# Scan decays of a two-layer hybrid step: running sums spread over the partitions by DMA and a minimum of two differences, in place of two triangular products

## The reference, cut to what matters

```
cs = jnp.cumsum((dt * A).reshape(b, nc, T, H), axis=2)
decay_in = jnp.exp(jnp.where(causal, cs[:, :, :, None, :] - cs[:, :, None, :, :], -jnp.inf))
y_diag = jnp.einsum('bclsh,bcshp->bclhp', cb * decay_in, xdt)
states = jnp.einsum('bclhn,bclhp->bchpn', Bh * jnp.exp(cs[:, :, -1:, :] - cs)[..., None], xdt)
```

## Time and profile before

| | |
|---|---|
| median of 3 runs | 1350.33 us (1347.05 to 1352.32) |
| the profiled execution | 1345.9 us, its span 1343.4 us |
| mean granted clock of TensorE | 0.974 of full |
| PE / DVE / ACT / POOL busy | 1214.7 / 457.9 / 328.4 / 210.2 us |

### The profile page before, as it was taken

The page is one execution under the profiler, slowest core; times in us unless marked ns, Lnnn a source line. Parts: engine busy times, 40 slices in busy tenths (PEclk is TensorE's granted clock), DMA queues, the critical chain, the costliest instruction groups (busy, mean ns, idle before and its releaser), DMA issues.

```text
span 1343.4 us, 16757 instructions
## 1 busy us (share of the span) xinstructions
PE 1214.7 (90%) x6414; PEld 682.4 (51%) x6414; DVE 457.9 (34%) x1019; ACT 328.4 (24%) x840; POOL 210.2 (16%) x269
## 2 busy tenths in 40 slices
PE   4999998999999999969999788999888969989787
PEld 2456654555545554446555444753455546555443
DVE  1442078543237760361111114122364351111114
ACT  4212364200022300231111113213353231111112
POOL 1000022200123601011122102052001011111201
PEclk9998999999999999969999999999999969999999
DMA  9995920576920128269999998860313479999994
GB/s 342 376 380 190 340 67 1 210 263 216 366 92 1 63 73 329 79 246 392 419 418 419 420 410 321 275 63 3 141 63 116 178 258 413 418 419 420 419 404 186
DMA packets 94306, 342.83 MB, mean 255 GB/s; under 512 B 12654, under 2 KB 16468, under 8 KB 69409
## 3 DMA queue, kind: packets, MB, share of 16 engines
q1 hardware_dynamic: 73680, 309.47, 58.9%
q0 software_dynamic: 13664, 25.47, 6.9%
q10 hardware_dynamic: 6897, 6.97, 1.5%
HBM read 340.05 MB, written 28.43 MB: 274 GB/s over the span
## 4 chain that ended last, share of the span: by engine, by line
PE 67%; DMA 18%; DVE 6%; issue 4%; ACT 2%; POOL 2%; SPq 0%; ACTq 0%; DVEq 0%; POOLq 0%
PE bank L888 59%; DMA ring<-in_moe_w_down_dram 9%; PE bank L892 5%; DMA ring<-in_moe_w_up_dram 3%; PE bank L919 2%; DMA expert_rows<-arena,scr 2%; DMA ring<-in_ev_w_in_dram 2%; DMA arena<-expert_rows 1%; DMA ring<-in_w_ada_dram 1%; POOL ring L2742 1%; POOL hT L2745 1%; ACT ring L2029 1%; POOL arena L2745 0%; PE bank L965 0%; DVE arena L2609 0%
## 5 line engine op out<-in xcount | busy, mean ns | idle before, releaser
L888 PE MATMUL bank<-ring,arena 128*64 128x256 f32 (+3 forms) x2592 | 428.7, 434 | 38.2 <-DMA ring<-in_moe_w_up_dram 14.4
L888 PEld LDWEIGHTS bank<-ring,arena 128*64 128x64 f32 (+1 forms) x2592 | 214.7, 145 | 218.7 <-issue 113.6
L888 PE MATMUL bank<-hT,ring 128*128 128x384 f32 (+4 forms) x960 | 299.1, 469 | 3.0 <-DVE hT L2158 1.7
L888 PEld LDWEIGHTS bank<-hT,ring 128*128 128x128 f32 (+1 forms) x960 | 176.4, 191 | 122.3 <-issue 16.0
L888 PE MATMUL bank<-arena 128*64 128x256 f32 (+8 forms) x856 | 138.7, 400 | 16.1 <-DVE arena L2500 8.1
L888 PEld LDWEIGHTS bank<-arena 128*64 128x64 f32 (+4 forms) x856 | 67.7, 150 | 67.6 <-issue 40.9
L2549 DVE TENSOR_TENSOR hT<-hT,bank 128x256 f32<-128x256 f32 x32 | 13.5, 421 | 249.9 <-ACT hT L1920 249.9
L1920 ACT ACTIVATE hT<-bank 128x256 f32<-128x256 f32 x32 | 12.3, 384 | 238.7 <-PE bank L888 238.7
L892 PEld LDWEIGHTS bank<-cst,hT 128*128 128x128 f32 x368 | 49.3, 195 | 41.9 <-issue 38.7
L892 PE MATMUL bank<-cst,hT 128*128 128x128 f32 x368 | 61.9, 305 | 6.5 <-DVE arena L2520 4.3
L2554 DVE COPY arena<-bank 128x512 f32<-128x512 f32 x32 | 22.1, 692 | 124.1 <-PE bank L888 104.6
(11 more groups left out here) (323 smaller groups left out, 1159.9 us busy)
## 6 DMA issues: line engine op xcount, KB each, us to landing
ring<-in_moe_w_up_dram SPq DMA_DIRECT2D x28, 2048.0 KB, 21.1
ring<-in_moe_w_down_dram SPq DMA_DIRECT2D x26, 2048.0 KB, 19.7
ring<-in_w_ada_dram SPq DMA_DIRECT2D x24, 2048.0 KB, 15.7
ring<-in_moe_w_gate_dram SPq DMA_DIRECT2D x24, 2048.0 KB, 22.5
ring<-in_ev_w_in_dram SPq DMA_DIRECT2D x10, 2048.0 KB, 12.7
arena<-in_moe_w_gate_dram SPq DMA_DIRECT2D x8, 2048.0 KB, 16.3
arena<-in_moe_w_down_dram SPq DMA_DIRECT2D x6, 2048.0 KB, 21.8
ring<-in_ev_w_out_dram SPq DMA_DIRECT2D x4, 2048.0 KB, 17.4
```

The lines of the kernel that those rows point to most:

```text
L888: return nc.tensor.matmul(out, lhsT, rhs, start=start, stop=stop_, skip_group_check=True)
```

## The change

The two triangular products, their bank E and the scaled triangles are gone. In their place:

- After z chunk 3 and token_tiles(0), PE makes the running sums once, six small products that put 16 heads on 16 partitions: for each direction d and chunk t, dta against upto or since (banks "cs"). ACT copies them to runs_out and issues two DMAs on its queue to a DRAM tensor runs (3, 2, 16, 128).
- SP, behind the four copies of zeros, issues for each of the 12 steps a load that spreads the sums of four heads and both directions over all 128 partitions (128 x 2 x 512 numbers, 512 KB each), into three buffers in turn. The first waits for the two DMAs and for xbc, the next two for the last use of the lent slot's block (z chunk 7), each later one for the step that last used its buffer.
- ACT copies minus the running sum at the partition's own position to `here` (3 small copies beside wt). ramps(n) is now eight ACT instructions in place that add `here` to the spread sums; each is the difference cs[l] - cs[s] of one direction and head.
- DVE takes the smaller of the two directions' differences (L2231's place in the order), and ACT the exponential of that, in SBUF. ACT's order is now exp(n), then ramps(1) at n = 0, take_state, ramps(n+2). ramps(0) moves from behind token_tiles(0) to behind wt, ahead of the silu of z chunk 7, and ramps(1) to behind exp(0).
- The sum mdec + m2 moves from DVE to POOL, which now does m2 and the sum for each step.
- Some semaphores are merged: one for both initial-state loads, one for the last gate and norm rows of the experts, and the small ones of dt.
- Banks of the scan are dealt anew, and places of two output stagings and of one scratch are moved.

```diff
@@ -160,14 +160,14 @@
                 for half in range(2):
                     job(("xtk", t, half), "act")
                 job(("btk", t), "act")
+                if t == 0:
+                    for d in range(2):
+                        job(("cs", d), "act")
             elif t == NT:
                 for t in range(NT):
                     job(("wt", t), "act")
     job(("cb", 0), "dve")
     for step in range(-1, len(QUADS)):
-        if step + 1 < len(QUADS):
-            t, q = QUADS[step + 1]
-            job(("E", t, q), "act")
         if step >= 0:
             t, q = QUADS[step]
             if q == 3 and t + 1 < NT:
@@ -459,6 +459,7 @@
         banks = [psum[:, i, :] for i in range(8)]
 
 
+        runs_d = nc.dram_tensor("runs", (NT, 2, HEADS, P), F32).ap()
         gates_d = nc.dram_tensor("gates", (2, 2, 2, D), F32).ap()
         rows_d = [nc.dram_tensor("rows%d" % l, (T, D), F32).ap() for l in range(2)]
         outs_d = [nc.dram_tensor("expert_rows%d" % l, (2 * T, D), F32).ap() for l in range(2)]
@@ -502,19 +503,22 @@
-        rfs, rbs = (area(11520, 4, P), lent[0]), (area(12032, 4, P), lent[1])
-        expEs, m2 = (area(12544, 4, P), lent[2]), area(13568, 4, P)
+        runs = [area(11520, 2, 512)] + [ring[:, SSD_SLOT * SLOT + 1024 * i:SSD_SLOT * SLOT + 1024 * i + 1024].rearrange("p (d m) -> p d m", d=2)
+                                        for i in range(2)]
+        decays, m2 = [x[:, 0, :] for x in runs], area(13568, 4, P)
+        runs_out = area(15616, 2, T)
-                 tuple(ring[:, SSD_SLOT * SLOT + 512 * i:SSD_SLOT * SLOT + 512 * i + 512] for i in (3, 4)))
+                 (area(12544, 512), ring[:, SSD_SLOT * SLOT + 2048:SSD_SLOT * SLOT + 2560]))
-        stouts = (lent[5], lent[3], lent[4], area(14080, 4, P))
+        stouts = (lent[5], area(12544, 4, P), lent[4], area(14080, 4, P))
+        here = scr[:, 96:192].rearrange("p (t n) -> p t n", t=NT)
@@ -856,6 +860,16 @@
                     for l in range(2):
                         for c in range(2):
                             sp.dma_start(outs_d[l][c * T:(c + 1) * T, :], K["k_zero"]).then_inc(S("blank"), 16)
+                    for n, (t, q) in enumerate(QUADS):
+                        if n == 0:
+                            sp.wait_ge(S("scan_out"), 16 * 2)
+                            sp.wait_ge(S("xbc"), KX)
+                        elif n < 3:
+                            sp.wait_ge(done, LAST_USE[LOADS[SSD_NEXT - NSLOT]] + 1)
+                        else:
+                            sp.wait_ge(S("mm"), n - 2)
+                        sp.dma_start(runs[n % 3], runs_d[t, :, 4 * q:4 * q + 4, :].rearrange("d h l -> d (h l)").partition_broadcast(P))\
+                            .then_inc(S("runs_in%d" % (n % 3)), 16)
                 if k == LOAD_AT[("ada", 0, 3)]:
                     sp.dma_start(block_view(("xbc", 0))[:, 4:8, :], block_source(("xbc", 0))[:, 4:8, :])\
                         .then_inc(S("full%d" % first_k), 16)
@@ -1054,8 +1068,14 @@
                     pe.wait_ge(S("xbc"), KX)
                 if Z_SCAN <= c < Z_SCAN + NT:
                     token_tiles(c - Z_SCAN)
+                    if c == Z_SCAN:
+                        pe.wait_ge(S("dta"), 1)
+                        for d, sums in enumerate((upto, since)):
+                            ps = open_bank("cs", d)
+                            for t in range(NT):
+                                last = mm(ps[0:HEADS, cols(t)], dta[:, t, d, :], sums, True, True)
+                            last.then_inc(done, 1)
                 elif c == Z_SCAN + NT:
-                    pe.wait_ge(S("dta"), 1)
                     for t in range(NT):
                         ps = open_bank("wt", t)
                         mm(ps[:, 0:HEADS], after, dta[:, t, 0, :], True, True)
@@ -1077,8 +1097,8 @@
                         ps = open_bank("st", d, g)
                         mm(ps[:, :], btok[:, d + 1, g * P:(g + 1) * P], xw[:, g * 512:(g + 1) * 512], True, True).then_inc(done, 1)
                 if i == 0:
+                    pe.wait_ge(S("sinit_in"), 32)
                     for d in range(2):
-                        pe.wait_ge(S("sinit_in%d" % d), 16)
                         for g in range(2):
                             ps = open_bank("sinit", d, g)
                             for c in range(4):
@@ -1091,14 +1111,6 @@
                 for g in range(2):
                     last = mm(ps[:, g * P:(g + 1) * P], xbcT[:, KD + g, tt], xbcT[:, KD + 2 + g, tt], True, True)
                 last.then_inc(done, 1)
-
-            def decays(step, t, q):
-
-                ps = open_bank("E", t, q)
-                rf, rb = rfs[step % 2], rbs[step % 2]
-                pe.wait_ge(S("rfb"), 2 * (step + 1))
-                mm(ps[:, :], after, rf.rearrange("p h l -> p (h l)"), True, False)
-                mm(ps[:, :], before, rb.rearrange("p h l -> p (h l)"), False, True).then_inc(done, 1)
 
             def state_terms(t, d):
                 took(pe, "sinit", 1, 1)
@@ -1140,8 +1152,6 @@
             chunk_scores(0)
             arrived(("hy", 0, 0))
             for step in range(-1, len(QUADS)):
-                if step + 1 < len(QUADS):
-                    decays(step + 1, *QUADS[step + 1])
                 hy_ahead(1 if step >= 0 else 2)
                 if step >= 0:
                     t, q = QUADS[step]
@@ -1467,7 +1477,7 @@
-                pe.wait_ge(S("gff_in"), 16 * (l + 1))
+                pe.wait_ge(S("rows_gff_in"), 16 * (2 * l + 1))
@@ -1488,7 +1498,7 @@
-                    pe.wait_ge(S("gfin_in"), 16)
+                    pe.wait_ge(S("rows_gff_in"), 48)
@@ -1752,21 +1762,23 @@
...
             def ramps(n):
                 t, q = QUADS[n]
-                for d, (dst, m) in enumerate(((rfs[n % 2], upto), (rbs[n % 2], since))):
+                act.wait_ge(S("runs_in%d" % (n % 3)), 16 * (n // 3 + 1))
+                for d in range(2):
                     for j in range(4):
-                        last = A_(dst[:, j, :], m, ACT.Copy, scale=dta[:, t, d, 4 * q + j:4 * q + j + 1])
-                    last.then_inc(S("rfb"), 1)
-
-            act.wait_ge(S("dta"), 1)
+                        at = runs[n % 3][:, d, j * P:(j + 1) * P]
+                        h = d * HEADS + 4 * q + j
+                        last = A_(at, at, ACT.Identity, bias=here[:, t, h:h + 1])
+                last.then_inc(S("ramped"), 1)
+
             act.wait_ge(S("xbc"), KX)
             for c in range(KD):
                 full(act, "z", c)
@@ -1780,14 +1792,22 @@
                     full(act, "btk", t)
                     A_(btok[:, t, :], bank("btk", t)[:, 0:2 * STATE], ACT.Copy).then_inc(taken["act"], 1)
                     if t == 0:
-                        ramps(0)
+                        for d in range(2):
+                            full(act, "cs", d)
+                            A_(runs_out[0:HEADS, d, :], bank("cs", d)[0:HEADS, 0:T], ACT.Copy).then_inc(taken["act"], 1)
+                        took(act, "cs", 1)
+                        for d in range(2):
+                            act.dma_start(runs_d[:, d].rearrange("t h l -> h t l"), runs_out[0:HEADS, d, :].rearrange("p (t l) -> p t l", t=NT))\
+                               .then_inc(S("scan_out"), 16)
                 elif c == Z_SCAN + NT:
                     for t in range(NT):
                         full(act, "wt", t)
+                        A_(here[:, t, :], bank("wt", t)[:, 64:96], ACT.Copy, scale=-1.0)
                         if t:
                             A_(eoff[:, t - 1, :], bank("wt", t)[:, 64:96], ACT.Exp)
                         A_(wexp[:, t, :], bank("wt", t)[:, 0:64], ACT.Exp).then_inc(taken["act"], 1)
-            ramps(1)
+                    took(act, "wt", NT - 1)
+                    ramps(0)
 
             def take_state(d):
                 for g in range(2):
@@ -1804,14 +1824,14 @@
                             A_(sent[:, 3 * i, g * 512:(g + 1) * 512], bank("sinit", i, g)[:, :], ACT.Copy).then_inc(taken["act"], 1)
 
             for n, (t, q) in enumerate(QUADS):
-                full(act, "E", t, q)
-                if n >= 2:
-                    act.wait_ge(S("mm"), n - 1)
-                A_(expEs[n % 2].rearrange("p h l -> p (h l)"), bank("E", t, q)[:, :], ACT.Exp).then_inc(taken["act"], 1)
+                act.wait_ge(S("dve_scan"), 2 * n + 1)
+                A_(decays[n % 3], decays[n % 3], ACT.Exp).then_inc(S("decayed"), 1)
+                if n == 0:
+                    ramps(1)
+                if STATE_AFTER.get(n - 1, 2) < 2:
+                    take_state(STATE_AFTER[n - 1])
                 if n + 2 < len(QUADS):
                     ramps(n + 2)
-                if STATE_AFTER.get(n - 1, 2) < 2:
-                    take_state(STATE_AFTER[n - 1])
             took(act, "y", NT - 1, 3)
             for k in range(KD):
                 A_(sqssd[:, k, :], szT[:, k, :], ACT.Square).then_inc(S("sq"), 1)
@@ -2228,15 +2248,15 @@
```

(25 more changed lines are left out.)

24 lines of the change are left out of this document (12 added, 12 removed).

## The result

The changed kernel takes **1364.76 us** in the median (1363.11 to 1368.18, 4 runs), the kernel before beside it 1351.32 (1347.05 to 1353.0, 4 runs): ratio 1.011, 95% interval 1.0086 to 1.0133. It is 13.4 us slower; forecast were 8.0. The time lies above the forecast's own range (1354 to 1363) and inside the wide one (1347 to 1367).

What follows compares the result with a forecast made beforehand. PE was taken to bound the whole, the scan being shared with DVE. Start 4.9, steps 1 to 3 0.5, steps 4 to 10 0.9 and clock 1.7 gave +8.0 us: 1358.3 on the median's scale, range 1354 to 1363 (wide 1347 to 1367).

Steps and rivals of the forecast that it cites:

- it lands at 172.0: Scan start: first spread load, queued behind the zeros ending at 171.0, lands at 172.0 us; bounds 167 and 173.
- ACT's new order: Scan start: ramps(0), exposed table loads and take_state before ramps(2) put step 1's multiplication at 187.8, +4.9 us.
- 1.5 if that cover is gone: Before the scan: six running-sum products take about 1.5 us on PE, costed at nothing because the next wait is later.
- Steps 1 to 3: Scan, 182.85 to 205.65 us: DVE loses some waits but gains turns with POOL; +0.5 us, bounds -1.7 and +2.
- Steps 4 to 10: Scan, 205.65 to 237.12 us: turns between DVE and POOL make 32.4 against 31.5; +0.9 us, bounds -3.2 and +2.5.
- The plain step of 4.35: Late scan step: 0.60 + 0.60 + 0.69 on DVE, 1.04 + 1.27 on POOL, two hand-overs of about 0.08 us.
- The loads ... don't bind: Loads of steps 3 to 11: landing in 3.9 us, their chain takes 7.8 us for two steps against 8.7.
- The clock, +1.7: PE idles more in the scan; one exposed clock dip in projections behind it or a chunk state, +1.7 us, bounds 0 and 8.
- At most about 9 us: Scan: DVE has 8.8 us of slack, so taking work from PE can win at most about 9 us.
- much slower: Rival, chance 0.15: PE stays at 1.2 GHz through most of the scan, 1366 us, or a load lands in 6 us, 1364.
- Cancels out: Rival, chance 0.25: turns in the scan cost nothing and no clock dip is exposed; change near 0, 1350.5 us.
- faster: Rival, chance 0.10: first spread load lands before 167, DVE runs the scan without a gap; 8.8 us less, 1341.5.

Runs made afterwards that it cites:

- e1: Changed kernel with SP issuing the four copies of zeros three ring loads earlier; median 1359.28 us, ratio 1.0041 to 1.0097.
- e11: Changed kernel with the four copies of zeros moved behind the scan, after ring load 25; median 1359.24 us, ratio 1.004 to 1.0086.
- e2: Changed kernel with the silu of z chunk 7 put ahead of ramps(0) on ACT; median 1363.44 us, ratio 1.0067 to 1.0149.
- e13: Kernel before with the six running-sum products added on PE at z chunk 3, result unread; median 1354.03 us against 1350.4, ratio 1.0012 to 1.0046.
- e7: Changed kernel with zeros three ring loads earlier and each spread load reading distinct addresses, decays not the reference's; median 1362.03 us.
- e3: Changed kernel with the sum mdec + m2 back on DVE; median 1368.57 us, ratio 1.0108 to 1.0194.
- e9: Changed kernel with zeros earlier, silu ahead of ramps(0), sum on DVE and loads from distinct addresses, decays not the reference's; 1361.27 us.
- e10: Kernel before with only the sum of the two weights moved to POOL (one merged semaphore beside it); median 1347.45 us, ratio 0.997 to 1.0001.
- e15: Kernel before with the sum on POOL, run again in more rounds; median 1347.91 us, ratio 0.997 to 0.9999.
- e4: Kernel before without its two triangular products per step, decays not the reference's; median 1351.91 us in 10 runs, ratio 1.0009.
- e12: Changed kernel with zeros behind the scan, silu ahead of ramps(0) and banks behind the scan dealt as before; 1360.40 us, before 1350.46.
- e6: Kernel before with only the banks behind the scan dealt as in the changed kernel; median 1353.46 us against 1350.13.
- e5: Changed kernel with the banks behind the scan dealt as in the kernel before; median 1366.47 us, ratio 1.0085 to 1.0153.
- e14: Changed kernel with the running-sum products one z chunk later, behind z chunk 4; median 1367.03 us, ratio 1.0093 to 1.0157.

## Why the prediction was wrong, and where it was right

The direction and the main places were right, the size was not: +8.0 against +13.4. On the scale of the two profiled executions the 17.2 us are 11.9 at the start, 0.0 in steps 1 to 3, 1.9 in steps 4 to 10, 0.3 in the Hyena part, 4.9 in the gap, less 1.3 behind it and 0.5 outside the span.

- **The step that failed: "it lands at 172.0 (bounds: 167 ... and 173)".** It landed at 179.16, outside the bounds. I took the 512 KB at the rate of the stretch before (387 GB/s), 1.3 us, and the last bytes of the zeros at 171 as the end of their effect. Both terms were too small. The last copy of zeros lands at 175.3 in the trace of before itself, and no spread load of any run lands in under 4.7 us (the 512 KB loads of the earlier trace rows take 3.9). These 7.0 us make the start 11.9 in place of 4.9. e1 and e11 show that it is the zeros: moved away, no load lands later than 8.4 and 6.9 us. Why the last copy lands 4 us after the bytes stop, and what share loads 1 and 2 have, the traces don't show.
- **ACT's new order** held row by row: additions of the triangle copies' pitch (2.44 for eight), both table loads exposed, take_state ahead of ramps(2). From the landing to exp(1) the forecast had 15.1 us, measured are 14.9. e2 took 1.6 us off at step 1.
- **The products of the sums at "1.5 if that cover is gone".** Covered in the changed kernel, as said; uncovered they are 3.2 (e13), since the clock dips in z chunk 7. I had seen no row for that.
- **Steps 1 to 3:** forecast +0.5, measured 0.0.
- **Steps 4 to 10:** forecast +0.9, measured +1.9. The plain step of 4.35 is 4.19 (e7). "The loads ... don't bind" was wrong: they land in 5.3 us and not in 3.9, ACT waits for them in every late step, and DVE waits for ACT in three, which the prediction had named as the sign that the loads bind. By the working's own sum that is 7.8 + 1.4 = 9.2 for two steps against 8.7. That they cost so little is because the turns stand at the same height (e3, e7, e9).
- **The GPSIMD Engine Reference of the Trainium skill (4.1 Engine selection)**, by which the move of the sum costs: the trace agrees on the duration (1.27 against DVE's 0.69), but the move wins (e10, e15): what it saves in steps 3 and 5 is more than the 0.5 us that the late steps lose. Its key points (8), on the shared interfaces: the trace agrees, 1.53 and 1.55 for 0.69 and 1.04.
- **The clock, +1.7** for a dip behind the scan: it isn't there in the changed kernel's trace. From step 11 to the last filter product it takes 232.1 us before and 232.4 after. The mechanism exists, though: e4 and e12, two of the 12 profiles without products in the scan, have just such a dip of 1.7 us. In the scan PE's clock did fall, to 0.84; how much of that is hidden was not tried alone.
- **Not in the sum at all: the bank deal.** The change's description had "banks of the scan are dealt anew", and I costed only the merged waits (rightly at nothing). 4.9 us in the trace, 3.3 in the median of e6; put back in the changed kernel (e5) it gains nothing in the median.
- **"At most about 9 us"** of gain from PE's work: the bound holds, and measured are 2.7 us in the scan and nothing in the total (e4).

Of the rivals, "much slower" with "a load lands in 6 us" came nearest. Its 1364 is the measured time by chance: it had the cost in the late steps, with slower additions and a slower sum, and most of it lay at the start. "Cancels out" and "faster" fell: even with the three costs mended (e12) the kernel is 0.48% to 0.99% slower. Of these 9.9 us, by the traces, 3.2 are the running sums' (e13) and 1.8 the start of step 0 behind z chunk 7 (6.6 us in e12, 4.8 in before: the minimum now stands between the additions and the exponential); 3.1 are in the steps, and 2.0 in the Hyena part, where e12 has a wait of 1.25 us for the small load and the dip behind it. That the four make 10.1 and the medians 9.9 is closer than single profiles can be trusted. The 2.7 us by which e7 is over e1 stay open.

## What to carry to other kernels

Work taken off one engine of a stretch that several share is worth little, however much it is: 20.6 us of PE gave 2.7 in the scan here, and even these were lost behind it to a wait and a lower clock. What replaces it costs wherever it lies on the path: transfers, waits, a longer chain on another engine. Before a transfer is put on the path, look at what stands ahead of it in its queue and price its landing by a row of such a transfer under the same load, from issue to landing, not by the mean rate; and read the end of a transfer from its landing, not from the last bytes. When a planner deals buffers in turn, a use more or fewer changes the deal for everything behind it: compare the plans. And try the parts of a change alone: the one that looked the most doubtful was the one that paid.

## What the runs showed of the hardware that I had not expected

- A load of 512 KB issued right behind four DRAM copies of 1.5 MB landed after 27.4 us. The last copy landed 4 us after the bytes stopped (175.2 against 171), the load 1.9 to 4.0 us behind it in five profiles, whether issued at 152 or at 170.4 (e14); in 172 to 177 us the engines were shown 0.89 busy at 95 GB/s.
- 512 KB spread over 128 partitions from one 4 KB piece, in packets of 2 KB, land in 5.2 us; the same size from distinct addresses in packets of 4 KB in 3.6. The two properties were not tried apart.
- With 1.5 us of small products added, a dense stretch 15 to 22 us later has a dip to half clock in 12 of 12 profiles, and in none of 5 without them.
- DVE's minimum of two SBUF inputs takes 1.53 us in place of 0.69 when it meets a POOL product.
- The granted clock fell from 0.98 to 0.84 in the scan when PE's share there went from 62.7 to 43.8 of 70 us.
- In the kernel before, PE's idle 2.35 us in the scan are followed by four products in 3.61 us in place of 1.98; with the sum on POOL PE idles 0.66 us there, the dip is gone, and step 5 is 1.5 us shorter (e10, e15).
